# Reordering the entry of the attention loop: query spread, last compressed-key sums, compressed softmax and key steps

## The chip, the cores and the metric

The kernel runs on one core of a Trainium2 chip. The metric is the device time of one execution in microseconds, here the median of three runs. All times inside an execution count from the first instruction of the profiled one.

## What is computed

One inference step of a two-layer decoder for 256 prompt tokens and 8 decoding sequences (264 tokens in all, d_model 1024, float32). Layer 0 has a state-space mixer, layer 1 a sparse attention; behind each mixer stand a layer norm, a mixture of 16 experts with two chosen per token, a second layer norm and a gated per-layer embedding. The change lies in the attention of layer 1:

```python
s_c = q . k_cmp - slope * dist             # compressed keys: one per block of 64 positions
p_c = masked_softmax(s_c, dist >= 0);  o_c = p_c . v_cmp
imp = p_c summed over the query heads of a group; idx = top_k(imp, 16)
o_s = masked_softmax(q . k_sel[idx] - slope * dist) . v_sel[idx]
o_w = masked_softmax(q . k_win - slope * dist) . v_win       # window of 512
o   = g0 * o_c + g1 * o_s + g2 * o_w;  return o @ w_out
```

k_cmp and v_cmp are weighted sums over blocks of 64 rows, with a softmax over the positions as weights. For the decoding sequences the past (1024 positions each) lies in pages of 128 rows that a page table picks; for the prompt there are only 4 blocks.

## The kernel before, in words

Each engine has one program in order; semaphores join them, and the order is written out by hand. The attention of layer 1 begins at line 1588. Its parts:

- **Projection.** TensorE makes 21 tiles of 128 outputs (loop at line 1764). ScalarE takes each out of PSUM (2010 to 2019: queries `qT`, keys and values `kvT`, gates `gT_`). Meanwhile the pages for the compressed keys of the eight decoding batches arrive in three slots. Per batch VectorE multiplies two of four quarters by the position weights (`weigh`) and GpSimd the other two (1748 to 1751), and VectorE sums all four (`add_up`, 2096 to 2101). The last sum of a batch raises the semaphore `c_used`; it frees the slot for the next transfer.
- **Query spread** (2116 to 2123). VectorE copies the decoding queries into the block-diagonal `qbd` with four copies; `q_ok` lets TensorE start `dec_keys(0)`. It stands after batch 6. Batch 7 is multiplied behind it, and summed only after the first two `soft` (2213).
- **Entry on TensorE** (1907 to 1940). score(0), dec_keys(0), transposes of values and gates, four products whose result nobody reads (1924), the compressed scores of the prompt (1928 to 1932, they wait for `kc_ok`), score(1), the block-diagonal compressed values (1935 to 1939), dec_keys(1).
- **The loop of pairs** (1942 to 1980). The prompt's attention has 32 units, a head with either the selected or the window keys, two units to a pair. For each unit: TensorE `score`, VectorE `soft` (adds the bias, negated maxima), ScalarE `exps`, VectorE `scale` (reciprocal of the row sum), GpSimd two multiplies, TensorE `turn` (three transposes), ScalarE takes the result, TensorE `values`. The score of pair p + 2 waits until both soft of pair p + 1 are done. Two pairs make an output tile, which `out_tile` takes. In between stands the decoding batches' work at fixed pairs: `dec_keys(j)` for j = 0 to 3 (selected keys, 16 matmuls each, filling half a row of scores two by two), `dec_small`, `dec_window`, `dec_values` and transposes.
- **Compressed softmax of the prompt.** VectorE adds the bias and subtracts the maximum before the loop (2223 to 2226), ScalarE takes the exponential (2064), VectorE normalizes at unit 0 (2232 to 2239) and raises `pc_ok`; TensorE transposes at the end of pair 0 (1975 to 1980), VectorE copies the result to `pct` at unit 1, and `values` begins each output tile with its product with `vci` (1805).
- **SyncE's queue** (1685 to 1743) in order: pages of batches 2, 4 and 6; constants; after `c_used` 6 the keys of step 0; after tile 16 window keys; page numbers read again; window keys; **after `c_used` 8** the keys of steps 2 and 3, then value pages and window values (1719 to 1726, each slot after its `kv_used`), the store of the new keys and values, and behind them the output weights (1728, 1730) and the first weights of the expert layer (1732 to 1743). ScalarE's queue issues batches 3, 5 and 7 and, after `c_used` 7, the keys of step 1.
- **What follows.** The output projection (1984 to 1996), then layer norm and router. ScalarE stores the normalized tokens to DRAM in three stores (1309, `r_rows`); GpSimd waits for all three and gathers the rows of an expert pair with an indirect DMA (1389); TensorE transposes them (1141) and the expert matmuls begin (1160). While TensorE waits there it works through products of the per-layer embedding (1060). SyncE loads each further weight (2 MB) when its buffer is released (112).

## Time and profile before

| | |
|---|---|
| median of 3 runs | 1039.96 us (1039.9 to 1041.25) |
| profiled execution | 1040.76 us |
| its span, first to last instruction | 1038.8 us |
| mean granted TensorE clock | 0.987 of full |
| busy: TensorE / VectorE / ScalarE / GpSimd | 95% / 47% / 32% / 18% |
| attention of layer 1, projection included | 545 to 757 us |
| entry of the loop, up to pair 2 | 617 to 655 us |
| expert stage of layer 1 | 783 to 1000 us |
| DMA, mean over the span | 330 GB/s |

A timeline row gives the start, the time to the end of the last of a merged group, the engine, the line, the operation, the tile written and those read, and the count. One matmul call on float32 stands as two records, so that `x16` at line 1826 is 8 calls. In brackets stand the idle time of the engine before the row and the instruction or transfer that ended it. In windows the granted clock is a share of full speed (1.00 is 2.4 GHz, 0.50 is 1.2 GHz).

### The profile page before, as it was taken

The page shows a single profiled execution, that of the slowest core. Times are in us where ns is not written, and L with a number is a line of the kernel's source. Part 1 is how long each engine was busy: PE and PEld are TensorE (multiplying, and loading weights), DVE is VectorE, ACT ScalarE, POOL GpSimd, SP SyncE. Part 2 cuts the span into 40 slices and gives each one's busy share as a digit, 9 for nine tenths or more (in the row PEclk, how much of TensorE's full clock was granted, in tenths as well). Part 3 has the DMA queues.
Part 4 walks back from the last instruction along what each step waited for, and adds up shares of the span by engine and source line. Part 5 has one row for each costly group of instructions (what it writes and reads, how often), then busy time and mean ns, then how long its engine had stood idle before and what let it go on. Part 6 is the DMA issues. An engine that isn't in the chain of part 4 may idle for free. (4 is left out here: it accounts for less than half of the span.)

```text
span 1038.8 us, 14986 instructions
## 1 busy us (share of the span) xinstructions
PE 987.6 (95%) x5189; PEld 616.5 (59%) x5189; DVE 493.2 (47%) x1418; ACT 335.2 (32%) x879; POOL 184.5 (18%) x201
## 2 busy tenths in 40 slices
PE   8999999899999999998999998979999999999996
PEld 6888776788744444443578864445874444444365
DVE  2889898772531111110479997671154111111046
ACT  3212888720451111111241014572045111112033
POOL 0000006321130000000245542342102000000042
PEclk9999999999999999999999997999999999999999
DMA  9963788769769999999846998859987999999974
GB/s 317 322 215 115 231 263 273 244 215 398 326 267 426 427 426 426 427 426 428 324 149 244 390 330 275 267 167 353 426 352 272 426 426 428 423 427 427 428 300 209
DMA packets 90145, 343.21 MB, mean 330 GB/s; under 512 B 15890, under 2 KB 53906, under 8 KB 73170
## 3 DMA queue, kind: packets, MB, share of 16 engines
q1 hardware_dynamic: 80074, 319.48, 79.3%
q10 hardware_dynamic: 7688, 18.39, 5.0%
q0 software_dynamic: 2304, 4.33, 1.2%
q8 instruction: 45, 0.74, 0.3%
q14 instruction: 34, 0.28, 0.1%
HBM read 331.56 MB, written 23.04 MB: 341 GB/s over the span
## 5 line engine op out<-in xcount | busy, mean ns | idle before, releaser
L1528 DVE TENSOR_TENSOR gates_and_hidden<-bank,gates_and_hidden 128x512 f32<-128x512 f32 x16 | 11.1, 691 | 307.7 <-PE bank L1179 307.7
L1179 PE MATMUL bank<-expert_ring,x_packed 128*64 128x512 f32 x320 | 116.7, 600 | 0.0
L1160 PE MATMUL bank<-expert_ring,x_packed 128*64 128x512 f32 x416 | 112.7, 593 | 1.2 <-ACT x_packed L1321 0.7
L559 PE MATMUL ss<-xT,expert_ring 128*128 128x264 f32 x384 | 89.3, 392 | 4.9 <-DMA expert_ring<-in_ssd_w_in 4.9
L559 PEld LDWEIGHTS ss<-xT,expert_ring 128*128 128x128 f32 x384 | 72.9, 192 | 18.7 <-DMA xT<-in_xT 4.5
L1160 PEld LDWEIGHTS bank<-expert_ring,x_packed 128*64 128x64 f32 x416 | 36.7, 137 | 72.7 <-issue 72.7
L1389 POOL DMA_INDIRECT x_rows_packed<-x_rows,slot_token_int x16 | 16.3, 1020 | 334.8 <-DVE gates_and_hidden L1493 289.5
L1773 PE MATMUL bank<-xT,expert_ring 128*128 128x264 f32 (+1 forms) x324 | 72.5, 386 | 0.3 <-PEq L1006 0.3
L1523 DVE TENSOR_TENSOR acc<-acc,bank 128x264 f32<-128x264 f32 x128 | 54.9, 429 | 36.6 <-PE bank L1216 34.8
L1201 PE MATMUL bank<-expert_ring,gates_and_hidden 128*64 128x512 f32 x256 | 70.8, 595 | 1.4 <-ACT gates_and_hidden L1350 1.4
L1773 PEld LDWEIGHTS bank<-xT,expert_ring 128*128 128x128 f32 (+1 forms) x324 | 60.3, 187 | 12.4 <-issue 1.0
L1216 PE MATMUL bank<-gates_and_hidden,y_slots 128*128 128x264 f32 x256 | 60.3, 388 | 1.8 <-issue 1.8
L571 PE MATMUL ss<-xT,expert_ring 128*128 128x264 f32 x256 | 61.2, 392 | 0.7 <-ACT expert_ring_b L437 0.7
L1272 PE MATMUL bank<-slot_onehot,expert_ring 128*128 128x266 f32 x256 | 58.5, 387 | 0.0
L571 PEld LDWEIGHTS ss<-xT,expert_ring 128*128 128x128 f32 x256 | 47.3, 190 | 13.3 <-issue 4.3
L1272 PEld LDWEIGHTS bank<-slot_onehot,expert_ring 128*128 128x128 f32 x256 | 48.5, 189 | 9.0
L1216 PEld LDWEIGHTS bank<-gates_and_hidden,y_slots 128*128 128x128 f32 x256 | 45.5, 189 | 13.9 <-issue 5.0
L1332 ACT ACTIVATE y_slots<-bank 128x512 f32<-128x512 f32 x32 | 19.1, 597 | 106.2 <-PE bank L1201 95.6
L667 PE MATMUL ss<-conv_out,expert_ring 128*128 128x264 f32 x224 | 51.6, 386 | 0.9 <-issue 0.9
L1350 ACT ACTIVATE gates_and_hidden<-bank 128x512 f32<-128x512 f32 x16 | 9.6, 597 | 130.3 <-PE bank L1186 130.3
L1179 PE MATMUL bank<-expert_ring_d,x_packed 128*64 128x512 f32 x96 | 44.5, 611 | 5.2 <-DMA expert_ring<-in_moe_w_up 5.2
L1201 PEld LDWEIGHTS bank<-expert_ring,gates_and_hidden 128*64 128x64 f32 x256 | 21.7, 137 | 44.6 <-issue 42.7
(421 smaller groups left out, 1822.9 us busy)
## 6 DMA issues: line engine op xcount, KB each, us to landing
expert_ring<-in_moe_w_gate SPq DMA_DIRECT2D x26, 2048.0 KB, 19.9
expert_ring<-in_moe_w_up SPq DMA_DIRECT2D x18, 2048.0 KB, 20.6
expert_ring<-in_moe_w_down SPq DMA_DIRECT2D x16, 2048.0 KB, 19.6
expert_ring<-in_ssd_w_in SPq DMA_DIRECT2D x9, 2048.0 KB, 9.2
expert_ring_b<-in_moe_w_gate SPq DMA_DIRECT2D x6, 2048.0 KB, 17.5
expert_ring_c<-in_moe_w_up SPq DMA_DIRECT2D x6, 2048.0 KB, 22.3
expert_ring_d<-in_moe_w_up SPq DMA_DIRECT2D x6, 2048.0 KB, 20.8
expert_ring_c<-in_moe_w_down SPq DMA_DIRECT2D x6, 2048.0 KB, 22.3
```

Of the source, the lines that this page charges most:

```text
L559: last = mm(pt[m % 4][:, 0:T], wc[:, k, ((m - 1) % 4) * P:((m - 1) % 4 + 1) * P], xT[:, k, :], start=k == 0, stop=k == KD - 1)
L571: last = mm(z_bank[:, 0:T], wc[:, k, (j % 4) * P:(j % 4 + 1) * P], xT[:, k, :], start=k == 0, stop=k == KD - 1)
L667: last = mm(o_bank[m][:, 0:T], w_row(k)[:, m * P:(m + 1) * P], cv[:, k, :], start=k == 0, stop=k == JX - 1)
L1160: last = mm(hb[0][s * CAP:(s + 1) * CAP, :], xg[:, k, s * CAP:(s + 1) * CAP], unit(6 * i + s)[:, k * FF:(k + 1) * FF], start=k == 0, stop= ...
L1179: last = mm(hb[1][s * CAP:(s + 1) * CAP, :], xg[:, k, s * CAP:(s + 1) * CAP], unit(6 * i + 2 + s)[:, k * FF:(k + 1) * FF], start=k == 0, s ...
L1201: last = mm(ob[2 + a][s * CAP:(s + 1) * CAP, :], ht[:, k, s * CAP:(s + 1) * CAP], unit(6 * i + 4 + s)[:, o:o + 512], start=k == 0, stop=k ...
L1216: mm(bank[:, 0:T], ys[:, d * P:(d + 1) * P], sgt[:, i, :], start=True, stop=True).then_inc(sc_done, 1)
L1272: last = mm(gate_bank[m % 6][:, 0:T + 2], wc[:, k, (m % 4) * P:(m % 4 + 1) * P], scaled[:, k, :], start=k == 0, stop=k == KD - 1)
L1332: A_(ys[:, a * 512:(a + 1) * 512], ob[2 + a][:], ACT.Copy).then_inc(ys_ok, 1)
L1389: nc.gpsimd.indirect_dma_start(xrow[:, i % 2, :], None, x_rows[L][:, :], bass.IndirectOffsetOnAxis(idxi[:, i:i + 1], 0), bounds_check=T - ...
L1523: V.tensor_tensor(acc[:, d, :], acc[:, d, :], bank[:, 0:T], ALU.add).then_inc(acc_ok, 1)
L1773: last = mm(pb[m % 8][0:M, 0:T], wc[:, k, (m % 4) * P:(m % 4) * P + M], xT[:, k, :], start=k == 0, stop=k == KD - 1, skip_group_check=m == 0)
```

## The change

- TensorE: seven unread products instead of four; dec_keys(1) moves from before the loop to pair 0, dec_keys(2) from pair 1 to 2, dec_keys(3) from pair 2 to 4. The transposes of the compressed probabilities move from the end of pair 0 to the end of pair 1. In `values` the compressed product stands in the second pair of a tile, between the two groups of matmuls, and no longer begins the tile; the wait for `pct_ok` 3 moves with it.
- ScalarE: the compressed exponential comes after exps(4) instead of before it.
- VectorE: the query spread stands before batch 6 instead of after it. The sum of the last quarter is split off (`add_last`); for batch 7 it comes after soft(2) and soft(3). The start of the compressed softmax moves behind soft(4) and scale(2), its second part from unit 0 to unit 2 (where the wait for the gates now stands), the copies of its transposes and of the small keys from unit 1 to unit 3.

```diff
--- before.py
+++ after.py
@@ -1797,16 +1797,16 @@
                     def values(pair):
                         i, v = pair // 2, pair % 2
                         ob = pt[4 + i % 2]
-                        if v == 0:
-                            if i == 0:
-                                pe.wait_ge(pct_ok, 3)
-                            if i >= 2:
-                                pe.wait_ge(ot_ok, i - 1)
-                            mm(ob[:, 0:SEQ], vci[:, i, :], pct[:], start=True, stop=False, skip_group_check=True)
+                        if v == 0 and i >= 2:
+                            pe.wait_ge(ot_ok, i - 1)
                         pe.wait_ge(pts_ok, 2 * pair + 2)
                         for half in range(2):
                             vw = slice(v * 256 + (2 * (i // 4) + half) * 64, v * 256 + (2 * (i // 4) + half) * 64 + 64)
-                            mm(ob[64 * half:64 * half + 64, 0:SEQ], vtok[:, 0, vw], pts[:, half, 0:SEQ], start=False, stop=False, skip_group_check=True)
+                            mm(ob[64 * half:64 * half + 64, 0:SEQ], vtok[:, 0, vw], pts[:, half, 0:SEQ], start=v == 0, stop=False, skip_group_check=True)
+                        if v == 1:
+                            if i == 0:
+                                pe.wait_ge(pct_ok, 3)
+                            mm(ob[:, 0:SEQ], vci[:, i, :], pct[:], start=False, stop=False, skip_group_check=True)
                         for half in range(2):
                             vw = slice(v * 256 + (2 * (i // 4) + half) * 64, v * 256 + (2 * (i // 4) + half) * 64 + 64)
                             mm(ob[64 * half:64 * half + 64, P:SEQ], vtok[:, 1, vw], pts[:, half, SEQ:3 * P], start=False, stop=v == 1,
@@ -1921,7 +1921,7 @@
                         last = tr(dp[1][0:DB, a * P:(a + 1) * P], kvT[:, t, SEQ:T], ident[:])
                     last.then_inc(pre_tr, 1)
 
-                    for _ in range(4):
+                    for _ in range(7):
                         mm(pt[4][:, 0:T], ident[:], xT[:, 0, :], start=True, stop=True)
 
                     pe.wait_ge(kc_ok, 2)
@@ -1937,13 +1937,12 @@
                             pe.wait_ge(vnew_ok, 1)
                         last = tr((pt[5], dp[1])[i // 4][0:64, (i % 4) * P:(i % 4 + 1) * P], vx[:, i * 64:(i + 1) * 64], ident[:])
                     last.then_inc(pre_tr, 1)
-                    dec_keys(1)
 
                     for pair in range(NU // 2):
                         if pair + 2 < NU // 2:
                             score(pair + 2)
-                        if 1 <= pair <= 2:
-                            dec_keys(pair + 1)
+                        if pair in (0, 2, 4):
+                            dec_keys(pair // 2 + 1)
                         if pair == 6:
                             dec_importance()
                         if 8 <= pair <= 9:
@@ -1972,7 +1971,7 @@
                         if 12 <= pair <= 13:
                             dec_values(2 * pair - 17)
                         turn(2 * pair + 1)
-                        if pair == 0:
+                        if pair == 1:
                             pe.wait_ge(pc_ok, 1)
                             pe.wait_ge(pct_ok, 1)
                             for q in range(QT):
@@ -2061,11 +2060,12 @@
                     A_(vci[:, 4:8, :], dp[1][0:64, :].rearrange("p (i m) -> p i m", i=4), ACT.Copy).then_inc(pct_ok, 1)
                     exps(2)
                     exps(3)
-                    act.wait_ge(cexp_in, 1)
-                    A_(pc[:], pc[:], ACT.Exp).then_inc(cexp, 1)
                     for u in range(NU):
                         if u + 4 < NU:
                             exps(u + 4)
+                        if u == 0:
+                            act.wait_ge(cexp_in, 1)
+                            A_(pc[:], pc[:], ACT.Exp).then_inc(cexp, 1)
                         if u == 9:
                             dec_exp(sc, 0, 1)
                         if u == 15:
@@ -2098,6 +2098,8 @@
                         cmp_sum(V, kcd, b, 1)
                         dve.wait_ge(c_mult, 2 * b)
                         cmp_sum(V, kcd, b, 2)
+
+                    def add_last(b):
                         cmp_sum(V, kcd, b, 3).then_inc(c_used, 1)
 
                     dve.wait_ge(ld_cmp[cmp_slot(0)], 16 * NPG)
@@ -2110,9 +2112,10 @@
                     V.memset(kcx[:], 0.0)
                     i1 = V.memset(vx[:], 0.0)
                     dve_step(dve, i1)
-                    for b in range(1, DB - 1):
+                    for b in range(1, DB - 2):
                         weigh(b)
                         add_up(b)
+                        add_last(b)
                     dve.wait_ge(q_zero, 1)
                     dve.wait_ge(tile_taken, t0 + KD)
                     for p in range(2):
@@ -2121,6 +2124,9 @@
                             i1 = V.tensor_copy(qbd[r, p, :].rearrange("q (b c) -> q b c", c=144)[:, :, 8 * p + 4 * half:8 * p + 4 * half + 4],
                                                qT[r, 4 * p:4 * p + 4, SEQ:T].rearrange("q r b -> q b r"))
                     i1.then_inc(q_ok, 1)
+                    weigh(DB - 2)
+                    add_up(DB - 2)
+                    add_last(DB - 2)
                     weigh(DB - 1)
                     dve.wait_ge(tile_taken, t0 + KD + 4)
                     for a in range(4):
@@ -2217,27 +2223,29 @@
                     bc = g(pst).unsqueeze(2).to_broadcast([P, QT * AH, 4])
                     soft(2)
                     soft(3)
-                    dve.wait_ge(gtok_ok, 1)
+                    add_last(DB - 1)
                     scale(0)
                     scale(1)
-                    dve.wait_ge(csc, 1)
-                    dve_step(dve, V.tensor_tensor(w(pc), pt[4][:, 0:QT * AH * 4], w(cbias), ALU.add))
-                    dve_step(dve, V.tensor_reduce(g(pst), f(pc), AX.X, ALU.max))
-                    V.tensor_tensor(f(pc), f(pc), bc, ALU.subtract).then_inc(cexp_in, 1)
                     for u in range(NU):
                         if u + 4 < NU:
                             soft(u + 4)
                         if u + 2 < NU:
                             scale(u + 2)
                         if u == 0:
+                            dve.wait_ge(csc, 1)
+                            dve_step(dve, V.tensor_tensor(w(pc), pt[4][:, 0:QT * AH * 4], w(cbias), ALU.add))
+                            dve_step(dve, V.tensor_reduce(g(pst), f(pc), AX.X, ALU.max))
+                            V.tensor_tensor(f(pc), f(pc), bc, ALU.subtract).then_inc(cexp_in, 1)
+                        if u == 2:
                             dve.wait_ge(cexp, 1)
+                            dve.wait_ge(gtok_ok, 1)
                             dve_step(dve, V.tensor_tensor(f(pc), f(pc), f(cmask), ALU.mult))
                             dve_step(dve, V.tensor_reduce(g(pst), f(pc), AX.X, ALU.add))
                             dve_step(dve, V.tensor_scalar(g(pst), g(pst), 1e-30, None, ALU.max))
                             dve_step(dve, V.reciprocal(g(pst), g(pst)))
                             dve_step(dve, V.tensor_tensor(pst[:], pst[:], g3[:, :, :, 0], ALU.mult))
                             V.tensor_tensor(f(pc), f(pc), bc, ALU.mult).then_inc(pc_ok, 1)
-                        if u == 1:
+                        if u == 3:
                             dve.wait_ge(pc_tr, 1)
                             V.tensor_copy(pct[:], pt[5][0:64, 0:SEQ]).then_inc(pct_ok, 1)
                             for p in range(2):
```

## Rows read from the trace of the kernel before

**Rows 1.** The chain of waits in order of time: start us, us, what.
```profile
772.38 4.43 DMA x_rows<-y_slots
...
777.67 3.40 DMA x_rows_packed<-x_rows,slot_token_int
...
783.46 7.09 PE bank L1160 x32
...
949.58 28.32 DMA expert_ring<-in_moe_w_up
```

**Rows 2.** Windows of 5 us: start:end, us, busy of five engines, granted clock, DMA share, GB/s.
```profile
765.00:770.00 5.00, 4.68 (x45) 3.91 (x38) 3.25 (x14) 3.60 (x7) 0.00 (x0) 1.00 0.99 423
775.00:780.00 5.00, 5.00 (x31) 4.38 (x29) 3.08 (x12) 0.78 (x2) 2.02 (x2) 1.00 0.15 34
```

**Rows 3.** DMA queues from 760 to 778 us: packets, MB, share of 16 engines.
```profile
q1 hardware_dynamic: 359, 5.10, 66.7%
q10 hardware_dynamic: 304, 1.08, 14.9%
```

**Rows 4.** Timeline of SyncE's DMA issues, 540 to 730 us: start us, us, engine, line, operation.
```profile
633.16 17.57 SPq L1677 DMA_DIRECT2D expert_ring<-in_ksel_pages  x32
650.83 16.06 SPq L1677 DMA_DIRECT2D expert_ring<-in_vsel_pages  x32
...
681.09 25.51 SPq L1677 DMA_DIRECT2D expert_ring<-in_vsel_pages  x32
...
709.43 0.45 SPq L1728 DMA_DIRECT2D expert_ring<-in_nsa_w_out  x1
```

**Rows 5.** Timeline of TensorE, 616 to 732 us; idle before and its releaser in brackets.
```profile
620.05 1.92 PE L1826 MATMUL bank<-expert_ring 128*32 128x512 f32 x16 [1.82 <-DVE expert_ring L2121]
...
623.62 1.95 PE L1925 MATMUL bank<-xT,ident 128*128 128x264 f32 x8
626.20 4.76 PE L1931 MATMUL bank<-cmp_prompt_pairs,expert_ring_b 128*128 128x8 f32 x32 [0.63 <-DVE gates_and_hidden L2136]
...
640.69 0.41 PE L1979 MATMUL bank<-ident,cmp_probs 128*64 128x128 f32 x2 [2.23 <-DVE cmp_probs L2239]
...
644.44 3.64 PE L1826 MATMUL bank<-expert_ring 128*32 128x512 f32 x16 [1.46 <-DMA expert_ring<-in_ksel_pages]
...
653.12 1.92 PE L1826 MATMUL bank<-expert_ring 128*32 128x512 f32 x16 [1.31 <-DMA expert_ring<-in_ksel_pages]
...
661.42 0.55 PE L1794 MATMUL bank<-ident,gates_and_hidden 128*128 128x128 f32 x3
...
728.36 4.02 PE L1995 MATMUL bank<-o_T,expert_ring 128*128 128x264 f32 x17 [0.46 <-issue]
```

**Rows 6.** A window of 1 us, columns as in rows 2.
```profile
648.00:649.00 1.00, 1.00 (x8) 0.66 (x4) 0.00 (x0) 0.00 (x0) 0.00 (x0) 0.50 0.80 248
```

**Rows 7.** Timeline of VectorE, 590 to 662 us.
```profile
608.02 4.51 DVE L136 TENSOR_TENSOR expert_ring<-expert_ring,pos_softmax 128x1024 f32<-128x1024 f32 x2 [2.38 <-DMA expert_ring<-in_cmp_pages]
...
617.08 2.91 DVE L2121 COPY expert_ring<-expert_ring_b 64x32 f32<-64x32 f32 x4
620.02 2.36 DVE L136 TENSOR_TENSOR expert_ring<-expert_ring,pos_softmax 128x1024 f32<-128x1024 f32 x2
...
626.17 0.55 DVE L2148 SCALAR_TENSOR_TENSOR gates_and_hidden<-expert_ring_b,bank 128x384 f32<-128x384 f32 x1
...
628.40 4.59 DVE L140 TENSOR_REDUCE cmp_dec<-expert_ring 128x16 f32<-128x1024 f32 x4
```

**Rows 8.** Line 2121, the query spread: durations in ns, least, median, most.
```profile
L2121 DVE COPY expert_ring<-expert_ring_b x4: 178/185/2320, 617.1 to 619.8; 64x32 f32<-64x32 f32 x4
```

**Rows 9.** Timeline of GpSimd, 600 to 640 us.
```profile
608.06 11.30 POOL L136 TENSOR_TENSOR expert_ring<-expert_ring,pos_softmax 128x1024 f32<-128x1024 f32 x4 [9.28 <-DMA expert_ring<-in_cmp_pages]
```

**Rows 10.** Timeline of TensorE, 757 to 800 us.
```profile
779.13 1.16 PE L1060 MATMUL bank<-gates_and_hidden 128*128 128x264 f32 x4
781.11 1.09 PE L1141 MATMUL bank<-ident,x_rows_packed 128*128 128x128 f32 x8 [0.83 <-DMA x_rows_packed<-x_rows,slot_token_int]
```

## The prediction

> **What bounds the kernel now.** Everything before the attention loop is untouched, so I asked three things: what ends the path behind the loop, what feeds it, and where the loop's entry waits.
>
> The chain of waits read in order of time [rows 1] shows how the second expert layer starts: the last store of token rows is issued at 772.38 and lands 4.43 us later, the gather of packed rows takes another 3.40, and the first expert matmul stands at 783.46. The chain's last long piece, 28.32 us at 949.58, is a weight transfer that the release of a buffer starts. So the expert stage moves with its first matmul, and that one with the landing of the row stores at 776.8.
>
> What do these stores wait for? The five-microsecond windows [rows 2] show the DMA engines full at 765 (423 GB/s) and nearly empty at 775 (34 GB/s). What fills them is the train of 2 MB weight loads that SyncE issues from the end of the attention loop on. From 760 to 778 its queue q1 takes 66.7% of 18 us, 12.0 us of all sixteen engines, and the row stores' queue q10 takes 14.9%, 2.7 us [rows 3]. Laid end to end that is done at 774.7; the landing at 776.8 is 2.1 us later. The row stores end behind the weight train, and not when TensorE lets them.
>
> Where does the train begin? SyncE's queue [rows 4] answers: 32 key pages from 633.16, 32 value pages from 650.83, after page numbers are read again 32 from 681.09, then window values, and the first output weight (L1728) at 709.43. The stretches follow one another: 633.16 + 17.57 is 650.73. This train of issues has no slack, and it starts when c_used reaches 8, that is with VectorE's last sum of batch 7.
>
> TensorE at the entry [rows 5] idles 1.82 us for the query spread, 0.63 for the compressed keys, 2.23 for the compressed softmax, and 1.46 and 1.31 for key pages. Its clock is at the lower level meanwhile: the keys at 644.44 take 3.64 us and the same 16 matmuls 1.92 at 653.12, and at 648 the granted clock is still 0.50 [rows 6].
>
> **The change, part by part.**
>
> *Query spread.* VectorE idles 2.38 us before batch 6 at 608.02; the spread took 2.91 at 617.08 [rows 7]. By shape it is four copies of 178 to 185 ns and one of them 2320 ns [rows 8]: that one ended at 619.4, with GpSimd's block of multiplies (608.06 + 11.30 = 619.36) [rows 9]. In the new place GpSimd is idle, so four copies cost some 0.75 us, inside the 2.38. Batch 6 is not later by it, and neither are the pages of step 1 that ScalarE issues behind c_used 7. But the next multiply meets the same GpSimd instruction: I let it start at 619.36, so the pair (2.36 us) ends at 621.72 instead of 622.38, a gain of 0.66 and not 2.91.
> The Trainium skill ("SBUF — State Buffer", section on the two separate sides) says that VectorE and GpSimd share a port pair that one holds for its whole instruction; the trace agrees by the 2320 ns copy. Without that rule the multiply would start at 617.1, and the gain would be 2.9 us.
>
> TensorE's keys of step 0 then follow score(0) at about 618.2 rather than 620.05 [rows 5]. Seven dummy products instead of four cost 3 x 0.49 = 1.46 us (1.95 us per 8 records). Their end is 625.57 - 1.85 + 1.46 = 625.2; the compressed keys are ready at 625.5. The third step is hidden behind that wait; were the cover gone it would cost 1.46. The compressed scores start at 625.5 instead of 626.20.
>
> *Last sums.* Three of four sums follow the first two maxima; two more maxima follow, each unit 1.12 us (626.17 to 628.40 for two) [rows 7]; then the fourth sum, a quarter of 4.59. The end moves from 632.99 by -0.66 + 2.23 to 634.56: **+1.57 us for everything in SyncE's queue**: the rest of the keys, all values, the kv store, the output weights, the weight train. The scales of units 0 and 1 still come half a microsecond sooner, since the softmax start (about 1 us) now stands behind them.
>
> *Compressed softmax.* Its start moves behind soft(4), its end behind soft(6), the transposes to the end of pair 1. What queues behind the new waits: soft(5) behind the scores (long ready), soft(7) behind the exponential (ready, since ScalarE issues it after exps(4)), score(4) on TensorE behind the transposes. TensorE now reaches its wait for pc_ok at some 641.2 with pair 1's work done, and the wait is about 0.8 us instead of 2.23. The same 16 compressed products are issued, only in the second half of a tile: nil. The copies of small keys move two units later; dec_small is at pair 3: nil, and a microsecond if it came early.
>
> *Keys.* dec_keys(2) and (3) move from pairs 1 and 2 to 2 and 4. In the trace the pages were in 11.3 us after SyncE's start (644.44 - 633.16) and 20 (653.12). Now: 646.0 and 654.7. dec_keys(1) goes to where TensorE waits for soft(3) anyway. VectorE, counted on from 634.56 (scales, soft(4), softmax start, soft(5), a wait for score(3), soft(6), the softmax's second part), has pc_ok ready at an estimated 641.9 and soft(7) at 643.0, so score(4) ends at 643.9, so dec_keys(2) waits about 2 us and ends at 647.9 (full clock, 1.92) or 649.6 (half, 3.64). Behind it pairs 2 to 4 hold an estimated 6.6 us up to dec_keys(3) (from 654.98, the end of the keys, to 661.42 the trace runs the same pieces of one pair less in 6.4 us), which starts at 654.7 to 656.2, and turn(8) at 656.7 to 658.1 against 661.42 [rows 5]. **TensorE leads by 3.4 to 4.7 us, I take 4.0.** Downstream of that the first output weight must be in: issued at 709.43 + 1.57 = 711.0, used at 728.36 - 4.0 = 724.4 [rows 4, 5], which leaves it 13.4 us; at 423 GB/s it and the 2 MB of window values ahead of it take some 10 us. So the lead can live to the end of the loop, though a larger one would meet this load.
>
> *What the lead buys.* Row stores issued 4.0 us sooner join a weight train that begins and ends 1.57 later. The DMA work ends at 774.7 + 1.57 = 776.3; of the 2.1 us between work's end and landing I keep 0.7, since the late issue of the third store, which made most of it, is gone (bounds 0 and 2.1: landing 776.3 to 778.4). Landing 777.0 instead of 776.8: **+0.2 us** (bounds -0.5 and +1.6).
>
> *Clock.* TensorE has fillers until 780.3, then 0.83 us of idle before the gathered rows [rows 10]. With a lead of 4.0 it idles about 5 us. After waits half as long the clock went to half [rows 5, 6], and after resuming at 644.44 it was half until 649, so 4.6 us of work at half, a cost of 2.3; the lower bound is nil. I take 1.2. This delays the first buffer release, which restarts the weight train: **+1.2 us**.
>
> Sum: the profiled execution was 1040.76 (span 1038.8), 0.80 above the median of 1039.96. 1040.76 + 0.2 + 1.2 = 1042.2, as a median **1041.4**.
>
> **Rivals.**
>
> 1. *The lead passes (faster).* The stores, issued 4.0 us sooner, slip between weight loads and land 4.43 us after issue as now. Then the index of the gather is sooner as well and the whole lead counts: 1039.96 - 4.0 = 1036.0. For it: the stores ride another queue than the weights. Against it: the stores took 4.43 us with the train ending, and here it doesn't end.
> The Trainium skill ("DMA: Bandwidth & Descriptors", section on queues, rings and completion order) says that each DMA engine takes turns between its queues packet by packet; by that rule the stores would share with the weights from their start, and whether they end before them depends on the sizes of the turns. No row here shows them in the middle of a train. Chance 0.22.
>
> 2. *Late pages decide (slower).* One place: c_used 8. If the weight train's +1.57 reaches the landing whole and the clock price comes on top, it is 1039.96 + 1.57 + 1.2 = 1042.7, with the clock's upper price 1043.8. It decides once the landing shifts by more than 0.9 us. For it: a queue of issues without slack. Against it: the 2.1 us that the landing now lags. Chance 0.18.
>
> 3. *No lead (no change to speak of).* The moved keys still stall TensorE until 655, since dec_keys(2) waits 2 us more and the clock falls there. Then the stores are issued as now, no extra idle arises, and the landing takes 0 to 1.57: 1040.0 to 1041.5. Chance 0.1.
>
> **How the numbers follow.** The forecast (lead on TensorE, swallowed by the DMA train, a small loss at the clock) has 0.50; its own range is 1039.5 to 1042.5. About 0.2% or 2 us is what a measurement here can tell from no change. Of the forecast 0.43 lies within and 0.07 above; rival 1 gives 0.20 faster and 0.02 within, rival 2 0.18 slower, rival 3 0.10 within. So faster 0.20, same 0.55, slower 0.25. The range for 8 in 10 takes in half of rival 1 and nearly all of rival 2: 1037.2 to 1043.8.
>
> **What the new profile would show.** Right: the four spread copies of about 0.2 us each before batch 6; the first multiply of batch 7 long, its end near 620.5; SyncE's 32 key pages starting 1.2 to 2 us later; turn(8) 3 to 5 us earlier and the output projection likewise; the last row store issued near 768.4 and taking some 8.5 us to land; TensorE idle for 4 to 6 us before L1141, with a granted clock of 0.50 around it. Wrong: row stores landing 4 to 5 us after issue (rival 1), or SyncE's pages not later than now, in which case the train ends sooner and the sum loses its positive terms; or a projection that starts at 728 as before (rival 3).

## The result, and the profile after

Over 20 executions each the changed kernel has a median of 1045.18 us, the kernel before 1041.17. The ratio is 1.0036, with a 95% interval of 1.0022 to 1.0049: it is slower, by 2.3 to 5.1 us, and above the range that was predicted. A ratio is not exactly the quotient of the two medians (1.0038 here); kernels are compared by the ratios. The 20 times reach from 1040.95 to 1050.14 us, before from 1038.32 to 1046.03. The profiled execution took 1041.52 us, the second shortest of its 20, so its page shows the change at its best. Set beside [rows 1], [rows 4] and [rows 5], the end of the path looks much as forecast, the start of SyncE's queue doesn't.

The chain of waits of the changed kernel, in order of time (start us, us, what), at the entry of the second expert stage:

```profile
769.48 1.14 ACT y_slots L1306 x2
...
770.64 6.02 DMA x_rows<-y_slots
...
777.51 3.37 DMA x_rows_packed<-x_rows,slot_token_int
780.92 1.75 PE bank L1141 x8
782.67 1.76 PE bank L1060 x4
784.43 7.12 PE bank L1160 x32
```

The last row store is issued 1.7 us sooner than in [rows 1] and lands at the same time, 776.66. The first expert matmul is 1.0 us later, since the transposes at L1141 and the fillers behind them run at half clock.

SyncE's issues in the changed kernel, 600 to 712 us (timeline):

```profile
633.00 17.23 SPq L1677 DMA_DIRECT2D expert_ring<-in_ksel_pages  x32
650.33 17.16 SPq L1677 DMA_DIRECT2D expert_ring<-in_vsel_pages  x32
...
681.57 26.31 SPq L1677 DMA_DIRECT2D expert_ring<-in_vsel_pages  x32
...
709.97 0.45 SPq L1728 DMA_DIRECT2D expert_ring<-in_nsa_w_out  x1
```

The queue starts at 633.00 as in [rows 4], where the forecast had it 1.2 to 2 us later, and reaches the first output weight 0.54 us later: from start to there it is 76.97 us long, before 76.27.

VectorE's timeline in the changed kernel (idle before and its releaser in brackets):

```profile
604.19 0.76 DVE L2124 COPY expert_ring<-expert_ring_b 64x32 f32<-64x32 f32 x4
606.40 4.52 DVE L136 TENSOR_TENSOR expert_ring<-expert_ring,pos_softmax 128x1024 f32<-128x1024 f32 x2 [1.45 <-DMA expert_ring<-in_cmp_pages]
610.95 4.60 DVE L140 TENSOR_REDUCE cmp_dec<-expert_ring 128x16 f32<-128x1024 f32 x4
615.46 4.51 DVE L136 TENSOR_TENSOR expert_ring<-expert_ring,pos_softmax 128x1024 f32<-128x1024 f32 x2
...
631.62 1.21 DVE L140 TENSOR_REDUCE cmp_dec<-expert_ring 128x16 f32<-128x1024 f32 x1
```

The spread takes 0.76 us in the page wait, as expected. Keep in mind that the margin to the pages is 1.45 us. The last sum ends at 632.83, 26.43 us after the multiplies of batch 6 begin; before it was 24.97 (608.02 to 632.99 [rows 7]). So the new order at the entry costs 1.46 us here, forecast 1.57, but the pages of batch 6 were in 1.62 us sooner in this execution, and that hides it.

TensorE's timeline in the changed kernel:

```profile
643.91 3.64 PE L1826 MATMUL bank<-expert_ring 128*32 128x512 f32 x16 [0.64 <-DMA expert_ring<-in_ksel_pages]
...
654.52 1.92 PE L1826 MATMUL bank<-expert_ring 128*32 128x512 f32 x16
656.37 0.55 PE L1794 MATMUL bank<-ident,gates_and_hidden 128*128 128x128 f32 x3
...
724.90 28.75 PE L1994 MATMUL bank<-o_T,expert_ring 128*128 128x264 f32 x128
...
764.87 2.84 PE L1091 MATMUL bank<-ident,xT 128*128 128x128 f32 x24
...
780.92 1.75 PE L1141 MATMUL bank<-ident,x_rows_packed 128*128 128x128 f32 x8 [2.38 <-DMA x_rows_packed<-x_rows,slot_token_int]
```

turn(8), at 656.37, is 5.05 us sooner than in [rows 5], the output projection 3.46 us, the last row store 1.74 us. A stretch at half clock in the router takes part of the lead back. The windows of the changed kernel (engines' busy us, granted clock, DMA share, GB/s):

```profile
755.00:760.00 5.00, 5.00 (x26) 4.32 (x25) 3.88 (x12) 3.45 (x9) 0.00 (x0) 0.73 1.00 423
...
780.00:785.00 5.00, 4.08 (x16) 2.91 (x18) 0.99 (x2) 3.15 (x10) 4.98 (x7) 0.66 0.26 71
```

So this profile is 1 us longer than the one before, and the medians differ by 4. The experiments had to find the rest.

### The profile page after: what moved, and what is told of

Its sections match the earlier page's. It is cut to its first block and busy times, and to the rows that moved or that the text cites. A ratio compares the mean times of both kernels' runs of the same rounds, so it can differ in the third digit from the quotient of the medians.

```text
span 1039.7 us, 15004 instructions
## 1 busy us (share of the span) xinstructions
PE 993.5 (96%) x5195; PEld 618.9 (60%) x5195; DVE 492.0 (47%) x1418; ACT 335.2 (32%) x879; POOL 184.9 (18%) x201
```

## The experiments

Each kernel has 12 executions (cmp_back 7, spread_caught 6, sum_keys_back 11), beside the kernel before on the same chip. "Undone" kernels start from the changed one, "only" and "before" kernels from the one before.

**The changed kernel again** (again, no edit).

> The changed kernel once more, to see the size of the loss on one chip beside the kernel before and a second profiled execution. Theory C (TensorE's clock): the loss is time at the lower clock; the runs of this kernel with a mean granted clock of 0.983 and less are the long ones, and the profile shows half-clock stretches at new places (757 to 761 and 781 to 785 in the first profile). Expected ratio to before 1.003 to 1.004, mean clock 0.98 to 0.985 against about 0.987. Theory P (late pages): the ratio is the same, but the weight train and the landing of the row stores are later by about 1.6 us or more in the profile, and the clocks of the two kernels don't differ.

Measured: 1045.96 us, ratio 1.0040 (1.0017 to 1.0062); mean granted clock of its executions 0.981, of those before 0.986. Long executions have the lower clock: in the 20 of the first measurement it was 0.979 in the five longest and 0.986 in the five shortest. That alone doesn't tell whether the clock makes them long or longer waits lower it. The profiled execution took 1049.38. VectorE's timeline in it:

```profile
605.07 9.20 DVE L2124 COPY expert_ring<-expert_ring_b 64x32 f32<-64x32 f32 x4
614.31 2.36 DVE L136 TENSOR_TENSOR expert_ring<-expert_ring,pos_softmax 128x1024 f32<-128x1024 f32 x2
...
635.62 0.56 DVE L2154 SCALAR_TENSOR_TENSOR gates_and_hidden<-expert_ring_b,bank 128x384 f32<-128x384 f32 x1 [2.57 <-PE bank L1785]
```

GpSimd's timeline in the same stretch:

```profile
604.97 9.27 POOL L136 TENSOR_TENSOR expert_ring<-expert_ring,pos_softmax 128x1024 f32<-128x1024 f32 x4 [6.66 <-DMA expert_ring<-in_cmp_pages]
```

The pages landed 0.1 us before VectorE came to the spread. GpSimd began its multiplies, and the four copies took 9.20 us instead of 0.76. TensorE's timeline behind that:

```profile
627.38 6.62 PE L1931 MATMUL bank<-cmp_prompt_pairs,expert_ring_b 128*128 128x8 f32 x32 [3.18 <-DVE gates_and_hidden L2142]
...
637.98 0.80 PE L1782 MATMUL bank<-expert_ring_c,expert_ring_b 64*128 64x128 f32 x4 [0.55 <-DVE neg_max L2156]
```

And SyncE's issues:

```profile
639.23 17.76 SPq L1677 DMA_DIRECT2D expert_ring<-in_ksel_pages  x32
...
717.37 0.45 SPq L1728 DMA_DIRECT2D expert_ring<-in_nsa_w_out  x1
```

The clock is at half during the compressed scores, so score(1) to score(3) are late, soft(2) waits 2.57 us for them, and the last sum behind it starts SyncE's queue 6.2 us later than in the first profile: soft(0) comes 3.6 us later (627.36 against 623.76), and the wait adds 2.57. The row stores land at 783.83.

**The spread caught always** (one wait more):

```diff
                     dve.wait_ge(tile_taken, t0 + KD)
+                    dve.wait_ge(ld_cmp[cmp_slot(DB - 2)], 16 * NPG * ((DB - 2) // 3 + 1))
```

> The changed kernel with one wait more: the spread waits until the pages of batch 6 have landed, so that GpSimd's multiplies start with it in every execution. Theory S (the spread is caught): the slow executions of the changed kernel are those in which the pages land before VectorE comes to the spread; the profile of the run again shows it, four copies in 9.20 us beside GpSimd's 9.27, against 0.76 in the first profile. Then all executions here are as slow as those: ratio to before 1.006 to 1.009, no execution near 1041, the copies 9 us in the profile, compressed scores on TensorE at 627 or later. Theory C (clock alone, random phase): a late spread costs VectorE a few us that TensorE's waits absorb, ratio 1.003 to 1.005.

Measured: 1051.66 us, ratio 1.0092 (1.0056 to 1.0129), shortest execution 1046.40. The spread in its VectorE timeline:

```profile
610.28 9.27 DVE L2125 COPY expert_ring<-expert_ring_b 64x32 f32<-64x32 f32 x4 [3.14 <-DMA expert_ring<-in_cmp_pages]
```

A caught spread is dear, and it is a matter of 1 to 2 us whether it is caught. The wait itself also makes VectorE later, by up to 3 us here, so 1.0092 is an upper bound for the catch.

**The spread safe, and the spread back.** spread_safe puts it between multiply and sums of batch 5; spread_back puts it behind batch 6, where it was:

```diff
                     for b in range(1, DB - 2):
                         weigh(b)
+                        if b == DB - 3:
+                            ...
                         add_up(b)
```

> The changed kernel with the spread between the multiply and the sums of batch 5, 2 to 5 us earlier, when GpSimd has finished batch 5 and the pages of batch 6 are still on their way. Theory S: never caught, the executions of 1046 to 1050 disappear, ratio to before 1.000 to 1.002. Theory C: as the changed kernel, 1.003 to 1.005.

> The changed kernel with the spread back behind batch 6, all else as changed. It is caught there too, but by 2.3 us at most. Theory S: ratio to before 1.000 to 1.0025, no execution over 1046.5. Theory C: 1.003 to 1.005. If the reordering behind the entry (last sum, compressed softmax, keys) costs by itself, it shows here as a ratio over 1.002.

Measured: spread_safe 1044.82 us, 1.0040 (1.0018 to 1.0061); spread_back 1046.51, 1.0051 (1.0026 to 1.0075). In spread_safe the copies take 0.78 us (VectorE's timeline):

```profile
598.60 0.78 DVE L2123 COPY expert_ring<-expert_ring_b 64x32 f32<-64x32 f32 x4
```

The theory missed: without a catch the loss is the same, so the median comes from the rest of the change. The catch can make an execution long; how often it happens in the changed kernel isn't shown.

**One other part undone.** sum_early puts the last sum back behind the third; keys_back puts dec_keys(1) before the loop, (2) and (3) at pairs 1 and 2; cmp_back puts the whole compressed softmax back; sum_keys_back undoes the first two together.

```diff
                     add_up(DB - 1)
+                    add_last(DB - 1)
...
                     soft(3)
-                    add_last(DB - 1)
...
-                        if pair in (0, 2, 4):
-                            dec_keys(pair // 2 + 1)
+                        if 1 <= pair <= 2:
+                            dec_keys(pair + 1)
```

> The changed kernel with the last sum of batch 7 back behind the third, ahead of soft(2) and soft(3); all else as changed. Theory P: c_used 8 comes some 2.2 us sooner, the key pages with it, and the time falls by 1.5 to 2.2 us against the changed kernel (ratio to before 1.0015 to 1.002). Theory C: SyncE's queue moves, the time hardly does: ratio to before 1.003 to 1.004.

> The changed kernel with dec_keys(1) before the loop and dec_keys(2) and (3) at pairs 1 and 2, as before; all else as changed. If TensorE's lead of 4 to 5 us is what brings the idle time and the half clock at the expert entry (theory C with the lead), the lead goes, turn(8) stands near 661 again and the ratio to before is 0.999 to 1.001. If the lead is worth nothing and costs nothing, the ratio stays at 1.003 to 1.004.

> The changed kernel with the compressed softmax in its old places (start before the loop, end at unit 0, transposes at the end of pair 0, the product at a tile's first half); spread, last sum, keys and dummies as changed. If moving it is what costs, the mean goes from about 1045.5 to 1042 or less (ratio to before under 1.002). Theory Q (the time is set by when SyncE's queue passes c_used 8 and by the clock at the expert entry, not by this part): no gain, ratio 1.003 to 1.006, since pair 0 then waits on TensorE for VectorE as before.

> The changed kernel with both the last sum early and the key steps at their old pairs; spread, dummies and compressed softmax as changed. Alone each took off 1 to 2 us of the mean. Theory Q: together nearly the whole loss, ratio 1.000 to 1.002, row stores landing about 777 and 6.6 to 8 us from there to the first expert matmul. If the softmax part or the dummies cost, the ratio stays over 1.003.

Measured: sum_early 1043.42 us, 1.0037 (1.0019 to 1.0055); keys_back 1043.43, 1.0031 (1.0012 to 1.0049); cmp_back 1044.50, 1.0050 (1.0028 to 1.0072); sum_keys_back 1043.26, 1.0022 (1.0006 to 1.0038), one execution of 1698.75 us left out. No single part carries the loss. Sum and keys together take off about half of it, though the intervals overlap.

**Fillers at the gather** (four unread products ahead of the wait for the gathered rows, layer 1 only), in the changed kernel and, with the spread safe and the sum early, in safe_sum_fill:

```diff
+                        if L == 1:
+                            for _ in range(4):
+                                mm(gb[0][:, 0:T], ones[:], pT[:, 0, :], start=True, stop=True)
                         turn_rows(0)
```

> The changed kernel with four more unread products (about 1.9 us) on TensorE before it waits for the gathered rows of layer 1, where the profile of the changed kernel shows 2.38 us idle and then the half clock until 784.6. Theory C: the clock stays at 1.00 there, L1160 begins about 0.9 us and the second half of its group 0.4 us sooner, the ratio to before falls by 0.001 to 0.0015, to about 1.0025. If the loss lies elsewhere: no change by more than 0.3 us.

> The changed kernel with the spread inside batch 5, the last sum early and the four products before the gather; keys, compressed softmax and dummies as changed. Theory Q: c_used 8 at about 631, landing to first expert matmul 6.6 us, ratio 0.998 to 1.001, the changed order without its three costs. If the moved keys or the softmax cost by themselves, ratio 1.002 or more.

Measured: fill_gather 1044.32 us, 1.0052 (1.0030 to 1.0074), although its profiled execution (1042.61) has the full clock at the expert entry and 6.6 us from landing to first expert matmul; the gain of a microsecond that the profile shows isn't seen in the median. safe_sum_fill 1041.51, 1.0021 (1.0003 to 1.0039).

**One part alone, added to the kernel before.** only_sum, only_keys and only_softmax are the three moves by themselves, each with its hunks of the change; before_spread and spread_again are the same kernel, with the spread in the page wait.

> The kernel before with the last sum of batch 7 behind soft(2) and soft(3), nothing else. c_used 8 then waits for TensorE's score(2) and score(3). My account of the entry: SyncE's queue starts at 634.9 to 636 instead of 633.2 and the row stores land as much later, ratio 1.0015 to 1.003. If the 2.1 us between the end of the weight train and the landing take it up: 0.999 to 1.001.

> The kernel before with dec_keys(1) at pair 0, (2) at pair 2 and (3) at pair 4, nothing else. Theory of the lead: TensorE reaches the out-projection 2 to 4 us sooner, idles at the expert entry, the clock falls there (landing to first expert matmul 7.7 to 8.8 us instead of 6.6): ratio 1.001 to 1.002. If SyncE's issue of values is slowed by it (S to the second value pages 48.6 to 50.9 us in most kernels with the moved keys, 47.0 to 47.9 in those without), another 1 to 2 us: 1.002 to 1.004. Nothing: 0.999 to 1.001.

> The kernel before with the compressed softmax, its transposes and its product moved as in the change, nothing else. TensorE's wait of 2.23 us before the transposes shrinks, TensorE is 1 to 2 us sooner at pair 2 and waits for pages there: ratio 0.999 to 1.001. As a cause of its own it would give 1.002 or more.

> The kernel before with only the spread moved ahead of batch 6. Theory S: two kinds of executions, most about like before or 1 us less, and some 3 to 6 us longer, so ratio 1.001 to 1.003 and a longest execution of 1046 or more. Theory C with its cause in the later order: ratio 0.998 to 1.000.

> The kernel before with only the spread ahead of batch 6, a second time, to narrow the interval. If the gain is real: ratio 0.997 to 0.999 again; two or three long executions in twelve where the spread is caught by GpSimd's multiplies.

Measured: only_sum 1042.85 us, 1.0012 (0.9994 to 1.0030); only_keys 1043.28, 1.0018 (0.9997 to 1.0039); only_softmax 1043.21, 1.0008 (0.9986 to 1.0029); the spread 0.9985 (0.9965 to 1.0005) and 0.9991 (0.9967 to 1.0014). None is certain by itself.

In only_sum VectorE waits for TensorE ahead of the last sum (its timeline):

```profile
631.45 0.56 DVE L2151 SCALAR_TENSOR_TENSOR gates_and_hidden<-expert_ring_b,bank 128x384 f32<-128x384 f32 x1 [1.41 <-PE bank L1785]
...
633.68 1.21 DVE L140 TENSOR_REDUCE cmp_dec<-expert_ring 128x16 f32<-128x1024 f32 x1
```

SyncE's queue then starts at 635.06 (issues of only_sum):

```profile
635.06 16.68 SPq L1677 DMA_DIRECT2D expert_ring<-in_ksel_pages  x32
...
710.62 0.43 SPq L1728 DMA_DIRECT2D expert_ring<-in_nsa_w_out  x1
```

In only_keys TensorE starts the projection 3.40 us sooner than before and idles at the expert entry (its timeline):

```profile
724.96 28.72 PE L1994 MATMUL bank<-o_T,expert_ring 128*128 128x264 f32 x128 [0.46 <-issue]
...
784.37 1.97 PE L1141 MATMUL bank<-ident,x_rows_packed 128*128 128x128 f32 x8 [5.80 <-DMA x_rows_packed<-x_rows,slot_token_int]
786.13 1.91 PE L1060 MATMUL bank<-gates_and_hidden 128*128 128x264 f32 x4
```

The windows of only_keys show the granted clock there, 0.60 and 0.72 of full:

```profile
780.00:785.00 5.00, 0.63 (x3) 0.64 (x4) 1.02 (x2) 0.00 (x0) 4.29 (x5) 0.60 0.32 84
785.00:790.00 5.00, 5.00 (x21) 2.90 (x21) 0.00 (x0) 4.48 (x12) 3.96 (x6) 0.72 0.03 10
```

SyncE's issues in only_keys are slower:

```profile
632.62 17.77 SPq L1677 DMA_DIRECT2D expert_ring<-in_ksel_pages  x32
650.48 17.86 SPq L1677 DMA_DIRECT2D expert_ring<-in_vsel_pages  x32
...
682.96 26.78 SPq L1677 DMA_DIRECT2D expert_ring<-in_vsel_pages  x32
...
712.98 0.43 SPq L1728 DMA_DIRECT2D expert_ring<-in_nsa_w_out  x1
```

**The keys alone with fillers, and two versions meant to be faster.** keys_fill is only_keys with the four products at the gather; before_safe is the kernel before with the spread inside batch 5; before_safe_fill has the four products too.

> The kernel before with the three key steps moved and the four unread products ahead of the wait for the gathered rows. If the clock fall at the expert entry is the cost of the moved keys: no half clock from 778 to 790, landing to first expert matmul 6.6 to 7 us instead of 8.5, ratio 0.999 to 1.001. If SyncE's queue is the cost (value pages of the second group 49.4 us behind c_used 8 instead of 47.7): ratio 1.001 to 1.002.

> The kernel before with only the spread between the multiply and the sums of batch 5. c_used 8 at 629 to 632 instead of 633.2, but TensorE is not sooner than before behind the loop and stands at the expert entry with 0.8 us idle at most: landing sooner by 1 to 3 us, the first expert matmul by 0 to 1. Ratio 0.998 to 1.000; faster than 0.998 only if TensorE is carried along.

> The kernel before with the spread between multiply and sums of batch 5 and with four more unread products ahead of the wait for the gathered rows in layer 1. The spread alone gave 0.9985 in its exposed place. Theory Q: c_used 8 comes 0.7 to 3 us sooner than 633.2, the clock stays up at the expert entry (landing to first expert matmul 6.6 us), ratio 0.996 to 0.999, faster than both kernels. Rival: the lock only moves to batch 7's multiply and nothing is gained, 0.999 to 1.001.

Measured: keys_fill 1044.22 us, 1.0036 (1.0015 to 1.0057); before_safe 1041.65, 1.0013 (0.9992 to 1.0033); before_safe_fill 1041.94, 1.0010 (0.9990 to 1.0029). So the three moved key steps and four unread products, with nothing else of the change, cost as much as the whole change. Beside only_keys (1.0018) the products may have a part in it; in before_safe_fill, beside before_safe, they cost nothing that can be seen. The chain of waits of keys_fill shows what the lead is worth:

```profile
766.92 10.43 DMA x_rows<-y_slots
...
778.20 3.42 DMA x_rows_packed<-x_rows,slot_token_int
781.67 1.97 PE bank L1141 x8
```

The last store is issued 5.5 us sooner than in [rows 1] and lands at 777.35, 0.5 us later than there. TensorE waits 5.07 us even behind the four products, and the clock falls all the same, so this run doesn't tell what the keys cost at full clock. In before_safe_fill the products stood on the path: the stores landed at 774.5, and the first expert matmul came only at 784.5.

**What all profiles say together.** All 20 profiles can be cut at the same events: c_used 8 (SyncE's first key page behind it), the landing of the first output weight, the landing of the last row store, the first expert matmul, the end. In us:

```
                     c_used 8   to w_out   to row stores  to expert   to the end
                                landed     landed         matmul
before                 633.2      89.0        54.6          6.6         255.4
after                  633.0      88.7        55.0          7.7         255.3
again                  639.2      89.9        54.7          8.0         255.6
sum_early              632.4      92.9        54.7          8.8         255.7
spread_safe            632.3      91.0        55.2          8.0         256.5
only_sum               635.1      88.3        54.6          6.6         255.4
only_keys              632.6      90.8        56.1          8.5         255.9
keys_fill              631.0      90.3        56.0          7.7         255.7
keys_back              633.4      90.3        55.5          8.0         255.5
only_softmax           633.9      89.0        56.3          6.6         255.5
spread_again           631.7      89.7        55.4          6.7         255.5
11 with keys moved                90.3 mean   54.6 to 56.1   7.9 mean
9 with keys in place              88.9 mean   54.6 to 56.3   7.6 mean
```

Four things are to be seen. Landing to landing it is 54.6 to 56.3 us in every profile, with the last store issued anywhere from 45.2 us (spread_back) to 54.5 us (before_safe_fill) behind the output weight's landing. Up to 51.7 us the store waits 3.9 to 10.4 us for its landing. In five profiles it is issued later, 52.6 us and more behind, and lands 1.8 to 2.7 us after issue; there its own lateness may set the landing. The second piece differs by the place of the keys: 88.6 to 92.9 us with the keys moved, 88.1 to 90.3 without. Third, the half clock stands in the trace between 775 and 800 us in all eight profiles with moved keys and no fillers, in one of three with moved keys and fillers, and in none of nine with the keys in place.

The fourth is a second path to the expert entry. The gather needs the token numbers (slot_token_int), which come from the router, as well as the stores. In keys_back GpSimd's timeline shows them coming last:

```profile
781.44 1.09 POOL L1389 DMA_INDIRECT x_rows_packed<-x_rows,slot_token_int  x1 [21.79 <-DVE slot_token_int L1485]
```

There the output projection begins at 733.11, and the first expert matmul comes 8.0 us behind the landing at full clock. It is so in the five profiles with the late store, all with the keys in place (keys_back, before_spread, sum_keys_back, before_safe, before_safe_fill: 7.5 to 8.0 us, and 10.0 with the products on the path) and in none of the eleven with the keys moved. So a lead does save something, about 1.4 us in keys_back (8.0 against 6.6), in executions in which TensorE would be late; in the others it is lost in the wait for the landing. That is why the piece up to the expert matmul differs by only 0.4 us between the groups (7.9 and 7.6), half clock included; without the four kernels that have the products it is 8.1 and 7.2.

## Why the prediction was wrong

*Half of the mechanism was there.* TensorE's lead was 3.46 us at the output projection, forecast 4.0, but only 1.74 at the last row store; the stores landed at 776.66, forecast 777.0; from there to the first expert matmul it was 7.7 us instead of 6.6, so the clock cost 1.1, forecast 1.2. For the profiled execution the forecast was 1042.2 and it took 1041.52. That closeness is in part luck: SyncE's queue, forecast 1.57 us later, started at 633.00, by the prediction's own words a sign of being wrong, since the pages of batch 6 came 1.62 us sooner than before. Rival 1 (the lead passes) is refuted by keys_fill: 5.5 us sooner, landed no sooner. Rival 3 (no lead) did not come. The trace shows the row stores ending with the weight train; it doesn't decide how the queues take turns.

*The base.* The sum started from the three executions at hand, median 1039.96; over 20 the kernel before has 1041.17. So of the 3.8 us between forecast (1041.4) and measured (1045.18), 1.2 are the base. As a difference the forecast was +1.4 us, and measured +4.0.

*The step that failed* is the size of what the DMA train does with a late start: "of the 2.1 us between work's end and landing I keep 0.7". No profile shows such a reserve. From the first output weight's landing to that of the stores it was never less than 54.6 us, and that is what the kernel before has, so what is lost at c_used 8 or in SyncE's queue reaches the stores. Of the 1.57 us the prediction let 0.2 through; without a reserve the whole arrives. With the pages of batch 6 as late as before, the first profile would have had its queue start at 634.6 and its stores land at about 778.3 (an estimate: both plus 1.62), 1.5 later than before. only_sum shows it: a queue that starts 1.9 us later (635.06), shortened by 0.7 on the way, stores 1.2 us later, span 1.2 us longer (1040.0), ratio 1.0012 (not told from 1). This was rival 2, which had 0.18 and a time of up to 1043.8.

*Beside it, two numbers were taken as fixed that aren't, and one path was left out.* First, "the end moves to 634.56". soft(2) and soft(3) were costed by their own 2.23 us, with no wait; but they need score(2) and score(3) from TensorE, and the last sum now stands behind them. In only_sum that wait is 1.41 us, in again 2.57. SyncE's start hung on score(0) and score(1) before; now it hangs on score(2) and score(3) as well, and so on TensorE's clock at the entry. Second, the queue's length. I carried c_used 8's shift to its end unchanged; in the profiles with moved keys the piece up to the output weight is 1.4 us longer on average (90.3 against 88.9), with slower issues of value pages (17.86 us for 32 in only_keys, 16.06 in [rows 4]; 15.8 to 19.2 in the eleven profiles with the keys moved, 15.7 to 16.2 in the nine others). The issues of only_keys stand 0.47 us apart as before; the time is in single gaps of 1 us and more, of which it has two and the kernel before one. What makes them is open. Third, the prediction let the stores alone decide the gather and had no term for the token numbers, which in five profiles come after them.

One reading had a wrong reason: the scales of units 0 and 1 come sooner by the 0.66 us of the multiply, and not since the softmax start stands behind them; it did so before.

*The spread.* "Inside the 2.38" held for one execution. Its cover is a page wait whose end moves from one execution to the next (margin 1.45 us in the first profile, -0.10 in again). When the pages win, each copy lasts as long as one of GpSimd's multiplies. I had used the lock to price the old place and not the new one. Still, on balance the spread alone was 0.9985 and 0.9991, so it isn't what makes the change slower.

*Adding up.* The parts alone give -0.12% for the spread (mean of two), +0.12 for the sum, +0.08 for the softmax and +0.18 for the keys, or +0.36 by keys_fill; together +0.26 to +0.44%, measured 0.36 and 0.40. They add up, but only keys_fill is resolved from no change, and keys_back (1.0031) took off less than the keys should. So it is shown that the moved keys with the four products cost as much as the whole change; that the keys alone do, and that sum and softmax add to it, is likely and not shown. Piece by piece the profiles give the moved keys 1.5 us (1.4 up to the output weight, -0.3 from landing to landing, 0.4 at the expert entry), or 2.4 without the kernels that have the products; the two ratios give 1.9 and 3.7. No profile was taken of an execution near the changed kernel's median, so what makes up its 4 us stays open in its shares. The seven dummies were not tried alone. The "nil" for the softmax can't be told from +0.8 us.

No kernel of the study is shown to beat the one before; the spread alone comes nearest, and both its intervals contain 1.

## What to carry to other kernels

Before pricing a lead, look at what the stage behind it waits for: here a DMA train set the landing in fifteen of twenty profiles, and a store issued sooner landed no sooner there; the lead became idle time and, in nine of the eleven profiles that had it, a lower clock. It could save time only where the other path, the token numbers, came last. Look for both paths in more than one profile: the one of the kernel before shows only the first. A step put into a wait is free only while the wait is there; compare the margin in more than one execution, and ask what it meets if the transfer wins, above all on VectorE beside GpSimd. When work is moved ahead of the instruction that starts a queue, count the waits of that work too, since from then on the queue hangs on them.

## What the hardware showed unexpectedly

A small VectorE copy caught by GpSimd doesn't pay once but each time: the four copies in again took 2.28, 2.30, 2.29 and 2.30 us beside four multiplies of 2.35 us, one copy per multiply, where one takes 0.18 us alone [rows 8]. The Trainium skill ("SBUF — State Buffer", section on the two separate sides) speaks of a lock that one of the two engines holds for a whole instruction; the trace agrees, and here each of the four copies meets it anew. And the clock can fall with hardly any idle time before it: in the router of the changed kernel it was 0.73 of full from 755 to 760 with TensorE busy for all 5.00 us and 0.79 us idle ahead of that. In the kernel before the same 0.79 us of idle stand behind the same projection, and the clock stayed up (its windows):

```profile
755.00:760.00 5.00, 4.21 (x26) 3.47 (x24) 2.37 (x9) 0.04 (x1) 0.00 (x0) 1.00 1.01 429
```

So the idle time just before doesn't tell whether the clock falls.
